# A two-layer hybrid block: three projections multiplied tile by tile, low weight parts shared between VectorE and GpSimd

## The reference

```python
h   = rms_norm(x, norm_g) * (1.0 + scale[:, None]) + shift[:, None]
h_c = rms_norm(ctx, norm_g) * (1.0 + scale_c) + shift_c
(conv_val, conv_glu, conv_z, dq, dk, dv, dz, dbeta, ddecay,
 aq, ak, av, az, mgate) = jnp.split(h @ w_in, IN_SPLITS, axis=-1)
...
qkv = jax.nn.silu(depthwise_conv(jnp.concatenate([q, k, v], axis=-1), dn_conv_w))
q = l2_norm(q...); k = l2_norm(k...)
beta = jax.nn.sigmoid(beta_logit)
g = -jnp.exp(dn_a_log) * jax.nn.softplus(decay_logit + dn_dt_bias)
...
decay = jnp.where(lower, jnp.exp(g[..., :, None] - g[..., None, :]), 0.0)
a = jnp.where(strict, einsum(k_beta, k) * decay, 0.0) + eye      # delta rule, chunked
...
y = conv branch, delta branch, differential attention branch
x_new = x + gate * (sum_n sigmoid(mgate_n) * (y_n @ w_branch_n)) @ w_out
```

## Time and profile before

| | before |
|---|---|
| median of 3 runs | 2073.14 us (2070.95 to 2074.45) |
| profiled execution | 2072.0 us, span 2070.2 us |
| TensorE busy | 1841.0 us (89%) |
| weight loads busy | 1527.5 us (74%) |
| VectorE busy | 1076.6 us (52%) |
| ScalarE busy | 974.0 us (47%) |
| GpSimd busy | 851.9 us (41%), of it 601.3 us in the 420 halves of low parts |
| mean TensorE clock | 0.94 of full |

### The profile page before, as it was taken

How to read it: one execution, slowest core, us unless ns; L and a number is a source line. 1 busy time by engine, 2 the same in 40 slices (tenths; PEclk the granted TensorE clock), 3 DMA queues, 4 the chain that set the end, 5 groups by cost and what they waited for, 6 DMA issues and landing times. The chain is left out here.

```text
span 2070.2 us, 27795 instructions
## 1 busy us (share of the span) xinstructions
PE 1841.0 (89%) x11060; PEld 1527.5 (74%) x11060; DVE 1076.6 (52%) x1536; ACT 974.0 (47%) x1300; POOL 851.9 (41%) x638
## 2 busy tenths in 40 slices
PE   6879996999998989878898977989699989788989
PEld 5768886888877777767687865868697767666767
DVE  4656492568665464534123135648759765454122
ACT  6556524255344534533453245563336455444551
POOL 2133335555544343333367212344246534323473
PEclk9989997999999999989998998999899999999999
DMA  7123223412221222213234212224222212112343
GB/s 280 51 68 97 67 92 121 143 42 62 72 72 51 69 67 84 70 49 92 89 107 158 97 56 73 83 89 114 83 72 61 75 58 64 54 51 72 97 125 130
DMA packets 76415, 178.87 MB, mean 86 GB/s; under 512 B 6464, under 2 KB 29312, under 8 KB 76160
## 3 DMA queue, kind: packets, MB, share of 16 engines
q1 hardware_dynamic: 34272, 122.46, 19.5%
q10 hardware_dynamic: 42016, 54.63, 7.8%
HBM read 156.00 MB, written 21.07 MB: 86 GB/s over the span
## 5 line engine op out<-in xcount | busy, mean ns | idle before, releaser
L1879 POOL TENSOR_TENSOR wLs<-raw,wHs 128x512 fp32r<-128x512 f32 x420 | 601.3, 1455 | 832.0 <-ACT wHs L830 831.9
L465 PE MATMUL banks<-hH,wHs 128*128 128x512 f32 x1984 | 606.0, 367 | 60.6 <-DVE hL L433 20.4
L465 PE MATMUL banks<-hL,wHs 128*128 128x512 f32 x1984 | 586.8, 358 | 0.0
L465 PE MATMUL banks<-hH,wLs 128*128 128x512 f32 x1984 | 585.4, 357 | 0.0
L465 PEld LDWEIGHTS banks<-hH,wHs 128*128 128x128 f32 x1984 | 330.9, 194 | 135.0 <-issue 26.4
L465 PEld LDWEIGHTS banks<-hL,wHs 128*128 128x128 f32 x1984 | 329.7, 194 | 57.2 <-issue 2.6
L465 PEld LDWEIGHTS banks<-hH,wLs 128*128 128x128 f32 x1984 | 328.4, 193 | 55.8
L830 ACT ACTIVATE wHs<-raw 128x1024 fp32r<-128x1024 f32 x210 | 220.4, 1053 | 260.8 <-DMA raw<-wstream 260.6
L1449 DVE SCALAR_TENSOR_TENSOR acc<-padc,vecs,acc 128x783 f32<-128x783 f32 (+1 forms) x240 | 296.4, 1291 | 0.0
L819 ACT ACT_TABLE_LOAD x183 | 234.8, 1283 | 29.2 <-issue 11.9
L864 ACT ACTIVATE Pa<-banks,stat 128x768 f32<-128x768 f32 (+1 forms) x80 | 64.5, 812 | 134.1 <-DVE stat L1409 132.1
(11 more groups left out here) (241 smaller groups left out, 2430.4 us busy)
## 6 DMA issues: line engine op xcount, KB each, us to landing
raw<-wstream SPq DMA_DIRECT2D x210, 512.0 KB, 3.6
araw<-wstream SPq DMA_DIRECT2D x16, 512.0 KB, 12.5
E<-g_rows ACTq DMA_DIRECT2D x16, 384.0 KB, 6.6
egb<-eg_rows ACTq DMA_DIRECT2D x20, 256.0 KB, 4.1
inb<-intra_rows ACTq DMA_DIRECT2D x20, 256.0 KB, 4.6
parked_logits<-sg ACTq DMA_DIRECT2D x13, 384.0 KB, 4.1
xs<-xT SPq DMA_DIRECT2D x8, 384.0 KB, 11.4
intra_rows<-E ACTq DMA_DIRECT2D x8, 384.0 KB, 3.1
```

The source lines that it names most:

```text
L465: last = pe.matmul(out[:, a:b], w, m[:, kt, a:b], start=(kt == 0 and j == 0), stop=(kt == kts - 1 and j == 2))
L1879: ins = pool.tensor_tensor(wL[w % RING][:, o:o + 512], raw[w % RING][:, o:o + 512], wH[w % RING][:, o:o + 512].bitcast(F32), ALU.subtract)
```

## The change

The list of a layer begins with the first k, the gates and the first v. TensorE multiplies these three together, tile by tile (`three_by_tile`), so three products of two banks each are open while the tiles of h arrive. ScalarE, VectorE and GpSimd meet these items in the new order. `gturn` moves behind the second k, the transposes and sums of the first head (`vt`, `dsum`) behind the second v, and the first `decay` behind them. The low parts of some kinds of units (`low_on_vector`: 74 of the 210) are made by VectorE in one instruction of 128x1024, called from its items (`low`, up to two units ahead); the others stay on GpSimd. Calls of `low` stand in VectorE's items `ada`, `nh`, `gb`, `dqkv`, `glu`, `branch`, `gate`, `qunit`, `vunit`, `park`, `leafpark`, `z`, `aout` and `out`, ahead of the item's own work.

```diff
@@ schedule()
-        out += [("nh", l), ("gb", l)]
-        for h in range(NT):
-            out.append(("dqkv", l, h, "dk"))
-            out += [("vt", l, h - 1), ("dsum", l, h - 1)] * (h > 0)
-            out += [("dsil", l, h, "dk"), ("dqkv", l, h, "dv"), ("dsil", l, h, "dv")]
-            out += [("gturn", l)] * (h == 0)
-            out.append(("dqkv", l, h, "dq"))
-            out += [("dturn", l, h - 1)] * (h > 0) + [("dsil", l, h, "dq"), ("dsq", l, h)]
-            out += [("kq", l, h - 1)] * (h > 0)
-            out.append(("decay", l, h))
+        out += [("nh", l), ("dqkv", l, 0, "dk"), ("gb", l), ("dqkv", l, 0, "dv"), ("dsil", l, 0, "dk"),
+                ("dsil", l, 0, "dv"), ("dqkv", l, 0, "dq"), ("dsil", l, 0, "dq"), ("dsq", l, 0)]
+        for h in range(1, NT):
+            last = [("vt", l, h - 1), ("dsum", l, h - 1)]
+            out += [("dqkv", l, h, "dk")] + ([("gturn", l)] if h == 1 else last)
+            out += [("dsil", l, h, "dk"), ("dqkv", l, h, "dv")] + last * (h == 1) + [("dsil", l, h, "dv")]
+            out += [("decay", l, 0)] * (h == 1)
+            out += [("dqkv", l, h, "dq"), ("dturn", l, h - 1), ("dsil", l, h, "dq"), ("dsq", l, h)]
+            out += [("kq", l, h - 1), ("decay", l, h)]
...
+def low_on_vector(u):
+
+    return u[0] in ("gb", "dk", "dv", "dq", "cz", "branch2", "branch0", "wout") or u[0] == "ada" and u[1] == 0
...
@@ TensorE
-                last = dense(u, out, hH, hL, segs(ntok(u[1], kind)), KT, dep=("h", u[1]) if kind == "gb" else None)
+                last = dense(u, out, hH, hL, segs(ntok(u[1], kind)), KT)
                 last.then_inc(*tick("pe", "pe", u))
+
+            def three_by_tile(l):
+
+                three = [("dk", l, 0), ("gb", l, 0), ("dv", l, 0)]
+                outs = [product(pe, u, TOK) for u in three]
+                for u in three:
+                    pe.wait_ge(*done("hi", u))
+                    pe.wait_ge(*done("lo", u))
+                for kt in range(KT):
+                    pe.wait_ge(*done("h", l, kt))
+                    cc = slice(kt * P, kt * P + P)
+                    for u, out in zip(three, outs):
+                        i = WIDX[u] % RING
+                        for j, (w, m) in enumerate(((wH[i], hH), (wH[i], hL), (wL[i], hH))):
+                            for a, b in segs(TOK):
+                                last = pe.matmul(out[:, a:b], w[:, cc], m[:, kt, a:b], start=(kt == 0 and j == 0),
+                                                 stop=(kt == KT - 1 and j == 2))
+                        if kt == KT - 1:
+                            last.then_inc(*tick("pe", "pe", u))
...
-                elif k == "gb":
-                    unit(units_of(it)[0], "gb")
...
                     h, kind = it[2], it[3]
-                    unit((kind, l, h), kind)
+                    if h == 0 and kind == "dk":
+                        three_by_tile(l)
+                    elif h or kind == "dq":
+                        unit((kind, l, h), kind)
@@ VectorE
+            done_lo = [0]
+
+            def low(u, n):
+
+                while done_lo[0] < min(WIDX[u] + n, len(UNITS)):
+                    w = done_lo[0]
+                    v = UNITS[w]
+                    done_lo[0] += 1
+                    if not low_on_vector(v):
+                        continue
+                    dve.wait_ge(*done("hi", v))
+                    dve.tensor_tensor(wL[w % RING][:, :], raw[w % RING][:, :], wH[w % RING][:, :].bitcast(F32),
+                                      ALU.subtract).then_inc(*tick("dve", "lo", v))
...
                     W = TOK + 1 if n == TOK else SEQ
+                    low((kind, l, h), RING - 1)
...
@@ GpSimd
                     done_lo[0] += 1
+                    if low_on_vector(v):
+                        continue
                     pool.wait_ge(*done("hi", v))
```

More of the change, by code:

```diff
@@ L1485, in _ @@
                             dve.tensor_scalar(nlam[:, v:v + 1], nlam[:, v:v + 1], -lam0, None, ALU.add).then_inc(*tick("dve", "nlam", v))
+                    if l == 0 and m == 6:
+                        low(UNITS[0], RING - 1)
+                    for u in units_of(it):
+                        low(u, RING - 1)
                     if m:
@@ L1496, in _ @@
                 elif k == "nh":
+                    low(("dk", l, 0), RING - 1)
                     dve.wait_ge(*done("gs", l))
@@ L1511, in _ @@
                 elif k == "gb":
+                    low(units_of(it)[0], RING - 1)
                     dve.wait_ge(*done("gln", l))
@@ L1736, in _ @@
                     n = ntok(l, "glu")
+                    low(("val", l, t), RING - 1)
+                    low(("glu", l, t), RING - 1)
                     dve.wait_ge(*done("read", ("glu", l, t), 0))
@@ L1749, in _ @@
                     n = ntok(l, "gate")
+                    low(("branch%d" % n_, l, p), RING - 1)
                     for j in range(2):
@@ L1770, in _ @@
                 elif k in ("gate", "qunit", "vunit"):
+                    low(units_of(it)[0], RING - 1)
                     conv(l, 1)
+                elif k in ("park", "leafpark", "z"):
+                    low(units_of(it)[0], RING - 1)
                 elif k == "lnsum":
@@ L1837, in _ @@
                     n = ntok(l, "az")
+                    low(("az", l, h), RING - 1)
                     dve.wait_ge(*done("aors", l, h))
```

## The result

The changed kernel takes 2036.3 us (median; four runs, 2034.5 to 2041.2) against 2072.6 (2071.0 to 2074.5) for the one before: ratio 0.9828, 95% interval 0.9808 to 0.9848, faster by 36 us. The forecast was 2052, its range 2041 to 2071. So the sign was right and the size too small: 36 us where the sum gave 21. The profiled execution of the changed kernel is the slowest of its four, 2041.2 us (span 2039.4), so the two traces differ by 31 us and not by 36.

A forecast was written before the change was run, and what follows sets the result against it. The prediction took TensorE, busy 89%, as the bound, with its 229 idle us and lower-clock stretches in question. First heads, later heads, ada and merges summed to 20.9 us off 2072.0 (median 2073.1), giving 2052; range 2041 to 2071.

The forecast's parts named there:

- the hand-carried queue of the first heads: First delta heads, queues of three engines summed: 0 us gained in layer 0, 1.8 us in layer 1.
- the wait for `acc` in the merge of layer 1: Merge of layer 1: ScalarE waits 2.85 us for GpSimd's `acc` behind a low part; removing it gains 2.6 us.
- the relief of the later heads: Later heads: without GpSimd's low parts the chain gains 3.7 us a cycle; 2.9 us in layer 0, 3.7, 4.5, 2.0 in layer 1.
- the three stops of the first head: Layer 0's first head: TensorE stops 3.1 and 3.3 us behind VectorE's low parts and 5 us behind `pad3`.
- Conv steps of 1.0 us in all heads: VectorE's convs: sign that the forecast is right; steps still near 1.9 us would show it wrong.
- A first cycle of 28.7 us: Layer 1's later heads: the first cycle falls from 32.4 to 28.7 us, against 28.3 us of matmuls.
- The stop on `padc`: Layer 1's later heads: TensorE's stop of 3.5 us on VectorE's `padc` goes.
- The 18.0 us on the copy into `pad3`: Layer 1's delta-head cycles: five TensorE waits of 18.0 us on ScalarE's copy, which frees the next projection's bank.
- Ada: Ada stage: TensorE's stops of 6.01 and 2.50 us for GpSimd's low part shrink, 2.5 us gained in all.
- the product by tile brings TensorE 4.5 us in `nh`: Start of layer 0: three projections made together tile by tile end at 82.9 instead of 87.4 us.
- E: Rival: first heads gain 4 us each because clock and TensorE's lead hold, and merges gain more; 2042 us, chance 0.10.
- C: Rival: first heads cost about 9 us each because E and weight loads land later; 2072 us, no change, chance 0.09.
- D: Rival: in the first heads nothing of the gates' delay is absorbed; slower, 2085 us, chance 0.11.

The follow-up runs named there:

- R7: The changed kernel with the low parts of cz, the branches and wout back on GpSimd: 2047.3 us, ratio 0.9882.
- R1: The kernel before with the low parts shared and nothing else, old order and projections one after another: 2034.6 us, ratio 0.982.
- R3: The changed kernel with the three products made one after another (first k, gates, first v): 2028.7 us, ratio 0.9783.
- R2: The changed kernel with every low part on GpSimd, keeping the product by tile and the new order: 2070.9 us, ratio 0.999.

## Why the prediction missed

By the table the stages of the changed kernel give, forecast in brackets: start 0.7 (0), first head of layer 0 5.0 (0), its later heads 2.9 (2.9), ada 3.5 (2.5), attention -6.5 (0), merge of layer 0 1.4 (0.9), first head of layer 1 5.6 (1.8), its later heads 6.2 (10.2), scan and attention 4.0 (0), merge and out of layer 1 8.0 (2.6). The sum is 30.8 for 20.9; most of what is missing to the 36 us of the medians is that the profiled execution was the slowest of its four.

**The steps that failed** are three terms of the sum: the hand-carried queue of the first heads, 8.8 us too pessimistic; the wait for `acc` in the merge of layer 1, 5.4 us too small; and the relief of the later heads, 4.0 us too optimistic, which hid part of the other two. In the first two the mechanism was right and the size wrong. In the third the mechanism was wrong for one head in four.

In the first head the differences add up, because one queue sets them all: ScalarE's last gates step ended at 92.2 (94.0 carried), the second k's copy at 113.4 (116.5), the exp behind the DMA issues at 120.4 (125.1), and `PM` of head 0 started at 141.1 (146.8). Of these 5.7 us, 0.7 are the earlier start. In layer 1, counted from its own start 7.0 us earlier, `PM` comes at 1301.4 (1304.2) and the third v at 1312.4 (1316.2). The largest single difference in layer 0, 1.6 us, is the DMA issues: I put seven us of them behind the copy, one after another. In the program all six stand behind the pad copies of that k. ScalarE's queue begins to issue them while the work ahead of them still waits or runs. ACTq is the queue, ACT the engine:

```profile
110.97 0.40 ACTq L894 DMA_DIRECT2D E<-g_rows  x1
111.07 0.62 ACT L1061 ACTIVATE qT<-c 128x512 f32<-128x512 f32 x1
111.41 0.57 ACTq L894 DMA_DIRECT2D E<-g_rows  x1
111.59 1.04 ACT L854 ACTIVATE wHs<-raw 128x1024 fp32r<-128x1024 f32 x1
112.01 0.56 ACTq L894 DMA_DIRECT2D E<-g_rows  x1
112.54 0.36 ACT L1042 ACTIVATE pad<-banks 128x256 f32<-128x256 f32 x1
112.59 3.21 ACTq L894 DMA_DIRECT2D E<-g_rows  x1
112.80 0.59 ACT L1043 ACTIVATE pad<-banks 128x512 f32<-128x512 f32 x1
115.84 2.90 ACTq L1019 DMA_DIRECT2D eg_rows<-EGR  x2
118.78 1.28 ACT L843 ACT_TABLE_LOAD   x1 [5.39 <-issue]
```

The issues take 7.8 us and the engine stands still for 5.39. The earlier trace rows had the same overlap, an issue at 98.71 beside a silu, and I didn't use it.

In the merge I priced one wait, the 2.85 us of the earlier trace rows. But ScalarE waits for `acc` once per tile of cz, and each wait delays the next tile. In the kernel before:

```profile
1954.37 0.81 ACT L1260 ACTIVATE acc<-acc,vecs 128x512 f32<-128x512 f32 x1 [1.49 <-POOL acc L1993]
...
1966.65 0.81 ACT L1260 ACTIVATE acc<-acc,vecs 128x512 f32<-128x512 f32 x1 [1.77 <-POOL acc L1993]
...
1978.87 0.82 ACT L1260 ACTIVATE acc<-acc,vecs 128x512 f32<-128x512 f32 x1 [2.40 <-POOL acc L1993]
```

In the changed kernel the last of these waits is 0.28 us and the others are gone, and TensorE's stop shrinks by 5.06. The stop ahead of out grows by 1.32, so the stops give 3.7 of the 8.0 us. Most of the rest is TensorE's own time: the same matmuls of merge and out take 118.8 us before and 115.3 after, at a mean granted clock of 0.95 and 0.99. R7 has 119.9 us at 0.93, R1 115.2 at 0.99, so the clock goes with the low parts too; that it rises because the stops are gone is likely and not shown.

In the later heads I took three low parts per head off GpSimd and had all conv steps at 1.0 us. But beside a conv GpSimd makes the low part of a weight three units further on, and beside the fourth head's convs that is a `val` or `glu`, which stayed there. That this is what the second cycle lacks is argued from the steps and from the forecast's own price of 3.7 us a cycle; no run moves these low parts alone. Layer 1's two cycles and what follows them gave 4.1, 0.7 and 1.4 us, where the sum had 3.7, 4.5 and 2.0. In layer 0 the 2.9 us agree by luck: 1.7 of them lie ahead of the fourth head's v, and of what lies behind it the larger part is that an ada stop got 1.4 us shorter.

Point by point: the three stops of the first head, right. Conv steps of 1.0 us in all heads: right for three heads, wrong for the fourth. A first cycle of 28.7 us, right (28.3). The stop on `padc`, 3.5 us in the earlier trace rows, was counted as gone and is 4.2. The 18.0 us on the copy into `pad3` in the earlier trace rows are of the whole span and not of the two cycles, as the prediction reads them; in front of those cycles stand 2.3 and 4.2 us. Ada, right: its two stops went from 6.01 and 2.50 us to 4.65 and 1.04, 2.8 us for 2.5. That the product by tile brings TensorE 4.5 us in `nh` is about right (its three products end at 81.5, not 87.4) and worth nothing at the end of the head, which R3 shows: with it, 5.0 and 5.6 us, without it 11.1 and 13.5. Of the rivals, E (2042) was nearest; C and D didn't come: the gates' delay (their last step on ScalarE 14.6 us later) was absorbed as the sum said. The 4.0 us between the scan and the end of attention in layer 1 are not the change, since the profiles of R2 and R1 win as much there (4.4 and 3.8). The execution of before ran slower there: its 2084 matmuls took 403.5 us at a granted clock of 0.95, those of R2 399.9 at 0.96.

## What to carry to other kernels

Before adding up TensorE's stops in a stretch, find the queue that ends it. Where ScalarE's queue is the longest, a stop that is removed comes back one product later, and product time saved on TensorE is waited off. Where one engine is entered once per tile, price its wait per tile and not at the last one. Where one engine works some units ahead, ask which unit it has in hand beside each step, and not only which ones belong to that step. And test the parts of a change alone: here one part was worth the whole gain, and another took 7 us of it back.

## What the runs showed of the hardware

A two-input step of VectorE (128x769) took 1.02 us beside GpSimd's memsets, as alone, and 1.92 beside its subtractions; over the kernel, 18 places with reads instead of writes cost 20 us. A low part on VectorE takes 1.22 us alone and 2.49 in the changed kernel's trace where a square on GpSimd runs beside it. ScalarE's queue issues a DMA several instructions ahead of what its engine is executing (here from 110.97, ahead of a copy that starts at 112.80), so six issues of 7.8 us cost the engine 5.39. And one unchanged stretch of 620 us with about the same stops differed by 7 us between two executions; the granted clock is the difference seen (0.80 against 0.89 in one window of it).
